# Packing tokens for the experts: the 24 rows of the third token tile in two row groups and two banks

## The chip, the cores and the metric

The kernel runs on one core of a Trainium2 chip. The metric is the device time of one execution in microseconds (us); several executions are timed and their median is given.

## The reference

One inference step of a two-layer decoder trunk for a prompt of 272 tokens (16 learned ones and 256 given) and 8 sample tokens, together 280 tokens of 1024 features. Each layer has a mixer (layer 0: retention beside a state space model; layer 1: RWKV-7 beside latent attention), a normalisation, and then a mixture of 16 experts in 4 groups, each with 256 hidden features. All is float32. What the change touches is the mixture:

```
coarse = softmax(x @ w_coarse + b)            # 4 groups, the best one is taken
fine   = logits of that group's 4 experts      # the best two are taken
y      = sum over the two experts e of  weight_e * (silu(x @ gate_e) * (x @ up_e)) @ down_e
```

Each token is so sent to 2 of 16 experts.

## The kernel before, in words

The activations lie feature-major in `XT` (128 partitions, 8 feature blocks, 280 tokens). Tokens are cut into three tiles `TT`: 128, 128 and 24 rows.

Per layer `out_and_moe` (TensorE) does: the output projection, the normalisation sums, the router logits (line 1588), then a transposition of `XT` to token-major form (line 1596), which ScalarE copies from the banks to `XTM` (line 2178). `XTM` has three tiles of 128 rows; of the third only 24 rows hold tokens, and GpSimd clears the whole third tile beforehand (`rest_zero`, line 1154), for which ScalarE waits.

Meanwhile VectorE works out the picks: `PICK` is a token by expert table of zeros and ones (lines 2002 and 2004; the second signals `pick_ready`). TensorE multiplies it by a table of "row before column" (`before`, lines 1602 to 1607), so that each token gets its place in its expert's list of at most 64. VectorE turns that into `PLACE` (line 2009) and, for one group of experts at a time, into `DSP` (line 2015), a token by slot table of zeros and ones, by comparison with `iota`. `dispatch_ready` counts the groups.

Then come eight pairs of experts (`q` from 0 to 7). `pack(q, half)` (line 1612) gathers the tokens of the pair: for four feature blocks, and for each of three token tiles, one product of `XTM` (stationary, 128 tokens by 128 features) with `DSP` (moving, 128 tokens by 128 slots), summed in one bank of four blocks of 128 columns. VectorE copies the bank to `XG` (`packed`, line 2018). `gate_or_up` (line 1630) multiplies `XG` by the weights, two experts side by side in the two 64-column halves of the array. `weights_turned` (line 1640) transposes the weighted dispatch table, its third part with 24 rows. `hidden_turned` (line 1648) transposes the hidden features, `down` (line 1662) multiplies them by the last weights.

The order is written out by hand. Two packs come ahead of the first pair. For each pair: gate, up, `pack(q + 1, 0)`, `weights_turned(q - 1)`, `hidden_turned(q)`, `pack(q + 1, 1)`, `down(q)`. The weights come through SyncE's DMA queue, 1 MB each, into nine buffers. After the last pair, line 1690 sums the experts' outputs into the residual.

Banks: VectorE empties four banks (`V`), ScalarE the other four (`A`), each a ring. `claim` waits until the bank was emptied, `take` waits until it was filled, `close` signals it full. `s.do` waits for the instruction's own completion before the engine goes on. ScalarE's order in `moe` (line 2172) is: normalisation, the six copies to `XTM`, an exponential (line 2180, waits for `lc_shift`), another (line 2182, waits for `lf_diff`), then the activations of the pairs.

Of the kernel before, what the change touches and what calls it, by code (L numbers as in the profile page):

```python
# [27 lines left out]
P = 128  # L28
D = 1024
KD = D // P  # L30
# [27 lines left out]
CAP = 64  # L58
# [6 lines left out]
          ("retmask", RH * NPR), ("kdec", 3 * RH), ("gam", 1), ("selbh", NB * RH),  # L65
          ("strictT", P), ("inclT", P), ("m2T", P), ("m2N", P),
          ("off2", P), ("off4", P), ("off8", P), ("off16", P),
          ("scan", NPR), ("causal", P), ("curmask", 2 * NB), ("rank", 4), ("eps", 4), ("before", P), ("iota", CAP)]
COFF = {}
_o = 0  # L70
for _n, _w in CONSTS:
# [5 lines left out]
def const_table():  # L77
    c = {n: np.zeros((P, w), np.float64) for n, w in CONSTS}
    i = np.arange(P)
    c["ident"] = np.eye(P)  # L80
    c["ones"][:] = 1.0
    c["id64"] = (i[:, None] % 64 == np.arange(64)[None, :]).astype(float)
    c["blk"] = (i[:, None] // 64 == i[None, :] // 64).astype(float)
    for name, d in (("perm64", 64), ("perm32", 32)):
        for m in range(P):
            if m % d < d // 2:
                c[name][m + d // 2, m] = -1.0
            else:
                c[name][m - d // 2, m] = 1.0
    pos = np.concatenate([np.arange(NPR), np.full(NB, PAST)]).astype(np.float32)  # L90
    for d, names in ((64, ("cosd", "sind")), (32, ("cosr", "sinr"))):
        inv = (10000.0 ** (-np.arange(0, d, 2, dtype=np.float32) / np.float32(d))).astype(np.float32)
        ang = (pos[None, :] * inv[:, None]).astype(np.float32)[i % (d // 2)]
        c[names[0]], c[names[1]] = np.cos(ang.astype(np.float64)), np.sin(ang.astype(np.float64))
    logg = np.log1p(-np.exp2(-5.0 - np.arange(RH)))
    x = np.arange(NPR)
    diff = x[None, :] - i[:, None]
    c["retmask"] = np.concatenate([np.where(diff >= 0, np.exp(logg[h] * np.maximum(diff, 0)), 0.0) for h in range(RH)], 1)
    c["kdec"] = np.stack([np.exp(logg[h] * np.maximum(NPR - 1 - (128 * t + i), 0)) for t in range(3) for h in range(RH)], 1)
    h_of = (i // 4) % RH  # L100
    c["gam"] = np.exp(logg[h_of])[:, None]
    c["selbh"] = ((i[:, None] // 4 // RH == np.arange(RH * NB)[None, :] % NB) &
                  (h_of[:, None] == np.arange(RH * NB)[None, :] // NB)).astype(float)
    a, b = i[:, None], i[None, :]
    blk = a // WC == b // WC
    c["strictT"] = (blk & (a < b)).astype(float)
    c["inclT"] = (blk & (a <= b)).astype(float)
    c["m2T"] = ((a // 2 == b // 2) & (a < b)).astype(float)
    c["m2N"] = ((a // 2 == b // 2) & (b < a)).astype(float)
    for s in (2, 4, 8, 16):  # L110
        c[f"off{s}"] = ((a // (2 * s) == b // (2 * s)) & (a // s > b // s)).astype(float)
    c["scan"] = np.broadcast_to((x % WC != 0).astype(float), (P, NPR))
    c["causal"] = np.where(b <= a, 0.0, -BIG)
    c["curmask"] = np.where(i[:, None] // 32 + 4 * (np.arange(2 * NB)[None, :] // NB) == np.arange(2 * NB)[None, :] % NB, 0.0, -BIG)
    c["rank"] = np.broadcast_to(np.array([4.0, 3.0, 2.0, 1.0]), (P, 4))
    c["eps"] = np.broadcast_to(np.array([1e-5, 64e-5, 1e-6, 0.0]), (P, 4))
    c["before"] = (a < b).astype(float)
    c["iota"] = np.broadcast_to(np.arange(1, CAP + 1)[None, :].astype(float), (P, CAP))
    return np.ascontiguousarray(np.concatenate([c[n] for n, _ in CONSTS], 1).astype(np.float32))

# [97 lines left out]
def program(nc, a, outs):  # L218
    sems = {}

    with ExitStack() as ctx:
# [6 lines left out]
        def ev(name):  # L228

            if name not in sems:  # L230
                sems[name] = sem(name)
            return sems[name]
# [21 lines left out]
        def cst(name):  # L254
            o, w = COFF[name]
            return CST[:, o:o + w]
# [74 lines left out]
        SIL, HB, HT = part(0, 2, DE), part(512, 2, DE), part(1024, 2, 2, P)  # L331
        LG, RT = part(1536, 3, 20), part(1600, 10, 3, 16)
        PICK, COMB, PLACE, CNT = part(2080, 3, NE), part(2128, 3, NE), part(2176, 3, NE), part(2224, NE)
        XTM = part(2240, 3, KD, P)
        XG = part(5312, 2, KD, P)
        DSP = part(7360, 3, NE, CAP)
        DSPT = part(10432, NQ, NT)
# [807 lines left out]
        def odd_pool(pool, s):  # L1145
# [2 lines left out]
                pool.wait_ge(ev("ln_done"), KD * (2 * l + 1))  # L1148
                pool.tensor_scalar(RES[:, :, :], XT[:, :, :], ALPHA, None, ALU.mult).then_inc(ev("sum_start"), 1)

            def rest_zero(l):

                pool.wait_ge(*mark[f"out{l}"])
                pool.memset(XTM[:, 2], 0.0).then_inc(ev("rest_zero"), 1)

            def weighted(l):

                pool.wait_ge(ev("comb_ready"), l + 1)
# [12 lines left out]
                s.do(pool.tensor_tensor(dst, TS[:, :, 0], TS[:, :, 1], ALU.add), sem)  # L1171


            rest_zero(0)
            weighted(0)
            sum_start(0)

# [37 lines left out]
            for sm in range(NB):  # L1215
                for pg in range(NPG):
# [1 line left out]
                    if i >= EARLY_PAGES:  # L1218
                        page.append(pool.value_load(PTAB[0:1, i:i + 1], min_val=0, max_val=a["cache_krope"].shape[0] - 1))
                    pool.dma_start(CK[:, sm, pg, 256:288], a["cache_krope"][bass.ds(page[i], 1), 0].rearrange("o p c -> p (o c)")).then_inc(ev(f"cache_krope_in{sm}"), 16)  # L1220
            rest_zero(1)
            weighted(1)
            sum_start(1)

# [45 lines left out]
        def _(pe):  # L1270
# [275 lines left out]
            def out_and_moe(l, s_out):  # L1546
# [55 lines left out]
                for t, (c0, r) in enumerate(TT):  # L1602
                    for u in range(t):
                        pe.matmul(b[:, NE * t:NE * t + NE], cst("ones"), one(u), start=(u == 0), stop=False)
                    pe.matmul(b[:, NE * t:NE * t + NE], cst("before")[:r, :], one(t), start=(t == 0), stop=True)
                for t, (c0, r) in enumerate(TT):
                    ins = pe.matmul(b[:, 3 * NE:4 * NE], cst("ones")[:r, :], one(t), start=(t == 0), stop=(t == 2))
                close(V, ins, "places")
# [3 lines left out]
                def pack(q, half):  # L1612

                    pe.wait_ge(ev("dispatch_ready"), NG * l + q // 2 + 1)
                    b = V.claim()
                    for i in range(4):
                        for t in range(3):
                            ins = pe.matmul(b[:, P * i:P * i + P], XTM[:, t, 4 * half + i, :], DSP[:, t, 2 * q:2 * q + 2, :].rearrange("p e c -> p (e c)"),  # L1618
                                            start=(t == 0), stop=(t == 2))
                    close(V, ins, f"xg{l}")  # L1620

                def gate_or_up(q, ring, n, name):

# [76 lines left out]
        def _(dve):  # L1700
# [266 lines left out]
            def out_and_moe(l):  # L1967
# [37 lines left out]
                dve.wait_ge(dve_step, s.n[dve_step.name])  # L2005
                s.do(sub(r1[5], r1[4], r1[3]), ev("lf_diff"))

                b = V.take()
                s.do(dve.scalar_tensor_tensor(PLACE, b[:, 0:3 * NE].rearrange("p (t e) -> p t e", t=3), 1.0, PICK, ALU.add, ALU.mult))
                s.do(dve.tensor_copy(CNT, b[:, 3 * NE:4 * NE]), v_free)  # L2010
# [5 lines left out]
                    s.mark(ins, ev("dispatch_ready"))  # L2016

                def packed(q, half):
                    empty(XG[:, q % 2, 4 * half:4 * half + 4, :], 512)

                dispatch(0)
                s.do(dve.tensor_reduce(CNT[:, 0:1], CNT, AX.X, ALU.max))
# [66 lines left out]
        def _(act):  # L2089
# [81 lines left out]

            def moe(l):
                layer_norm(2 * l, "ln1_g", "ln1_b", l)
                act.wait_ge(ev("rest_zero"), l + 1)
                for t, (c0, r) in enumerate(TT):
                    for h in range(2):
                        b = A.take()
                        act.activation(XTM[:r, t, :, 64 * h:64 * h + 64], b[:r, 0:512].rearrange("r (p k) -> r k p", k=KD), ACT.Copy).then_inc(a_free, 1)
                act.wait_ge(ev("lc_shift"), l + 1)
                act.activation(RT[:, 2, :, 0:4], RT[:, 2, :, 0:4], ACT.Exp).then_inc(ev("lc_exp"), 1)  # L2180
                act.wait_ge(ev("lf_diff"), l + 1)
                act.activation(RT[:, 5, :, 8:9], RT[:, 5, :, 8:9], ACT.Exp).then_inc(ev("lc_exp"), 1)
                for q in range(NQ):
# [155 lines left out]
```

## Time and profile before

| | us |
|---|---|
| median of 3 runs | 1191.88 (1188.89 to 1192.0) |
| profiled execution | 1186.78 |
| its span | 1185.1 |
| TensorE busy, matmuls | 1011.8 |
| VectorE busy | 495.1 |
| ScalarE busy | 202.6 |

The profile is of one execution. A busy matmul row overlaps with its neighbours, because matmuls are pipelined: each of them lasts some 0.28 us, while the next one starts 0.11 us after it. Weight loads (PEld) run beside matmuls. A product of two float32 operands shows as two loads and two matmuls.

### The profile page before, as it was taken

The page shows a single profiled execution, that of the slowest core. Times are in us where ns is not written, and L with a number is a line of the kernel's source. Part 1 is how long each engine was busy: PE and PEld are TensorE (multiplying, and loading weights), DVE is VectorE, ACT ScalarE, POOL GpSimd, SP SyncE. Part 2 cuts the span into 40 slices and gives each one's busy share as a digit, 9 for nine tenths or more (in the row PEclk, how much of TensorE's full clock was granted, in tenths as well). Part 3 has the DMA queues.
Part 4 walks back from the last instruction along what each step waited for, and adds up shares of the span by engine and source line. Part 5 has one row for each costly group of instructions (what it writes and reads, how often), then busy time and mean ns, then how long its engine had stood idle before and what let it go on. Part 6 is the DMA issues. An engine that isn't in the chain of part 4 may idle for free.

```text
span 1185.1 us, 17689 instructions
## 1 busy us (share of the span) xinstructions
PE 1011.8 (85%) x7132; PEld 766.8 (65%) x7132; DVE 495.1 (42%) x1056; ACT 202.6 (17%) x418; POOL 139.8 (12%) x179
## 2 busy tenths in 40 slices
PE   6998477778999999899747778889888888999995
PEld 4785365556867667688537678755455667667674
DVE  1796723453411111321587575584753235111104
ACT  0121001202210110301510000013355032110103
POOL 0004001000130000000026800000730002200000
PEclk9995756789799999999868889688599987999998
DMA  9402202525099994152000000010731541999501
GB/s 313 168 2 27 41 1 76 221 72 217 4 355 389 372 361 138 37 142 76 2 10 1 38 2 3 2 41 21 226 87 47 199 181 40 357 385 373 232 1 37
DMA packets 77203, 156.81 MB, mean 132 GB/s; under 512 B 19596, under 2 KB 57539, under 8 KB 68196
## 3 DMA queue, kind: packets, MB, share of 16 engines
q1 hardware_dynamic: 67650, 148.28, 34.4%
q0 software_dynamic: 3760, 4.48, 1.7%
q10 hardware_dynamic: 5710, 2.90, 0.9%
q8 instruction: 58, 0.95, 0.3%
q14 instruction: 25, 0.20, 0.1%
HBM read 149.18 MB, written 5.27 MB: 130 GB/s over the span
## 4 chain that ended last, share of the span: by engine, by line
PE 72%; DVE 21%; issue 2%; ACT 2%; DMA 2%; SPq 0%; DVEq 0%
PE bank L1630 9%; PE bank L1304 9%; PE bank L1618 8%; DVE scratch L1714 8%; PE bank L1690 5%; PE bank L1662 5%; PE bank L1557 5%; DVE scratch L1717 2%; PE bank L1418 2%; PE bank L1365 2%; PE bank L558 2%; PE bank L744 2%; PE bank L1588 2%; PE bank L1506 1%; PE bank L569 1%
## 5 line engine op out<-in xcount | busy, mean ns | idle before, releaser
L1304 PE MATMUL bank<-x_fm,weight_slots 128*128 128x280 f32 x576 | 140.9, 408 | 3.4 <-ACT x_fm L2170 2.8
L1304 PEld LDWEIGHTS bank<-x_fm,weight_slots 128*128 128x128 f32 x576 | 111.8, 195 | 31.0 <-issue 2.9
L2102 ACT ACTIVATE scratch<-bank 128x280 f32<-128x280 f32 (+5 forms) x136 | 60.9, 454 | 398.8 <-PE bank L1304 110.8
L1711 DVE COPY scratch<-bank 128x512 f32<-128x512 f32 (+5 forms) x92 | 57.6, 627 | 100.3 <-PE bank L1618 73.1
L1618 PE MATMUL bank<-scratch 128*128 128x128 f32 x768 | 95.8, 283 | 3.5 <-issue 3.5
L1618 PEld LDWEIGHTS bank<-scratch 128*128 128x128 f32 x768 | 91.6, 198 | 9.0 <-issue 9.0
L1630 PE MATMUL bank<-weight_slots,scratch 128*64 128x256 f32 x672 | 92.5, 379 | 1.7 <-DVE scratch L1711 1.7
L1630 PEld LDWEIGHTS bank<-weight_slots,scratch 128*64 128x64 f32 x672 | 58.6, 137 | 28.2 <-issue 4.6
L1714 DVE TENSOR_TENSOR scratch<-bank,scratch 128x256 f32<-128x256 f32 (+1 forms) x20 | 8.6, 430 | 141.2 <-PE bank L1630 140.6
L1557 PE MATMUL bank<-scratch,weight_slots 128*128 128x280 f32 x256 | 63.3, 410 | 4.9 <-DVE scratch L1714 4.9
L1714 DVE TENSOR_TENSOR scratch<-scratch 128x64 f32<-128x64 f32 (+13 forms) x97 | 60.4, 641 | 15.5 <-ACT scratch L2102 13.0
L1690 PE MATMUL bank<-scratch 128*128 128x280 f32 x256 | 60.9, 400 | 1.4 <-ACT scratch L2102 1.4
L1557 PEld LDWEIGHTS bank<-scratch,weight_slots 128*128 128x128 f32 x256 | 50.0, 196 | 17.6 <-DVE scratch L1714 5.3
L1690 PEld LDWEIGHTS bank<-scratch 128*128 128x128 f32 x256 | 48.5, 190 | 14.7 <-ACT scratch L2102 3.2
L1630 PE MATMUL bank<-scratch 128*64 128x256 f32 x352 | 56.9, 379 | 0.0
L1220 POOL DMA_DIRECT2D scratch<-in_cache_krope x64 | 34.3, 536 | 162.9 <-DVE residual L994 145.5
L1630 PEld LDWEIGHTS bank<-scratch 128*64 128x64 f32 x352 | 35.7, 137 | 16.4 <-issue 3.4
L1662 PE MATMUL bank<-weight_slots,scratch 128*64 128x512 f32 x192 | 43.8, 598 | 0.3
L1418 PE MATMUL bank<-scratch 64*42 64x128 f32 x128 | 25.9, 418 | 18.9 <-DVE scratch L1717 18.9
L1714 DVE TENSOR_TENSOR scratch<-bank,consts 128x512 f32<-128x512 f32 (+5 forms) x69 | 33.7, 488 | 14.9 <-PE bank L558 11.7
L2163 ACT ACTIVATE scratch<-residual 128x280 f32<-128x280 f32 x32 | 11.7, 437 | 157.4 <-DVE residual L1960 157.4
L1490 PE MATMUL bank<-scratch,consts 128*128 128x280 f32 x58 | 21.5, 540 | 18.8 <-DVE scratch L1714 17.8
(370 smaller groups left out, 1467.5 us busy)
## 6 DMA issues: line engine op xcount, KB each, us to landing
weight_slots<-in_moe_w_down SPq DMA_DIRECT2D x24, 1024.0 KB, 8.9
weight_slots<-in_moe_w_up SPq DMA_DIRECT2D x22, 1024.0 KB, 7.5
weight_slots<-in_moe_w_gate SPq DMA_DIRECT2D x20, 1024.0 KB, 6.2
scratch<-in_moe_w_gate SPq DMA_DIRECT2D x12, 1024.0 KB, 8.1
scratch<-in_moe_w_up SPq DMA_DIRECT2D x10, 1024.0 KB, 8.1
weight_slots<-in_od_w_in SPq DMA_DIRECT2D x9, 1024.0 KB, 5.3
weight_slots<-in_ev_w_in SPq DMA_DIRECT2D x8, 1024.0 KB, 11.6
scratch<-in_moe_w_down SPq DMA_DIRECT2D x8, 1024.0 KB, 9.4
```

The source lines that it names most:

```text
L558: ins = pe.matmul(heads(b, r)[:r, hp, :], NTM[:r, par, hp, 0:r], TM_[:r, par, hp, 0:r], start=True, stop=True)
L1220: pool.dma_start(CK[:, sm, pg, 256:288], a["cache_krope"][bass.ds(page[i], 1), 0].rearrange("o p c -> p (o c)")).then_inc(ev(f"cache_krope ...
L1304: ins = pe.matmul(b[:, 0:NT], w[:, k, P * m2:P * m2 + P], src[:, k, :], start=(k == 0), stop=(k == kt - 1))
L1418: ins = pe.matmul(b[0:HCOL, P * i:P * i + P], HS[lo:lo + SP_N, j, g // 2, :], CP[lo:lo + SP_N, j, g // 2, 1:CL + 1, :].rearrange("p l c -> ...
L1557: ins = pe.matmul(b[:, 0:NT], w[:, k0 + k, P * m2:P * m2 + P], src[:, k, :], start=(which == 0 and k == 0), stop=(which == 1 and k == 3))
L1618: ins = pe.matmul(b[:, P * i:P * i + P], XTM[:, t, 4 * half + i, :], DSP[:, t, 2 * q:2 * q + 2, :].rearrange("p e c -> p (e c)"), start=(t ...
L1630: ins = pe.matmul(b[CAP * j:CAP * j + CAP, 0:DE], XG[:, q % 2, k, CAP * j:CAP * j + CAP], w[j][:, k, :], start=(k == 0), stop=(k == KD - 1))
L1662: ins = pe.matmul(b[CAP * j:CAP * j + CAP, :], HT[:, q % 2, f, CAP * j:CAP * j + CAP], w[j][:, f, 512 * h:512 * h + 512], start=(f == 0), ...
L1690: ins = pe.matmul(b[:, 0:NT], YG[:, q, P * m:P * m + P], DSPT[:, q, :], start=(q == 0), stop=(q == NQ - 1))
L1711: s.do(dve.tensor_copy(dst, src if len(dst.shape) == 2 else src.rearrange("p (a b) -> p a b", a=dst.shape[1])), v_free)
L1714: return dve.tensor_tensor(o, x, y, ALU.mult)
L2102: return act.activation(dst, b[:rows, 0:width], f, **kw).then_inc(a_free, 1)
```

## The change

The third tile's 24 rows now lie twice, in partitions 0 to 23 and 32 to 55, in `XTM3`: the first copy holds two of each four feature blocks, the second the other two. `pack` claims two banks, and two 24-row products (one per row group, one per bank) start the sums; the four 128-row products of the two banks follow. `PICK` is copied to partitions 32 to 55, the constant table `before32` gives their places, and VectorE waits for that copy (`pick_spread`) before it computes `PLACE`. `packed` empties two banks of 256 columns. The clearing by GpSimd is gone.

```diff
     c["before"] = (a < b).astype(float)
+    c["before32"] = (a < b % 32).astype(float)
...
-        XTM = part(2240, 3, KD, P)
+        XTM, XTM3 = part(2240, 2, KD, P), part(4288, 2, 2, P)
...
-            def rest_zero(l):
-
-                pool.wait_ge(*mark[f"out{l}"])
-                pool.memset(XTM[:, 2], 0.0).then_inc(ev("rest_zero"), 1)
...
-                    pe.matmul(b[:, NE * t:NE * t + NE], cst("before")[:r, :], one(t), start=(t == 0), stop=True)
+                    pe.matmul(b[:, NE * t:NE * t + NE], cst("before32" if t == 2 else "before")[:r, :], one(t), start=(t == 0), stop=True)
...
-                    b = V.claim()
-                    for i in range(4):
-                        for t in range(3):
-                            ins = pe.matmul(b[:, P * i:P * i + P], XTM[:, t, 4 * half + i, :], DSP[:, t, 2 * q:2 * q + 2, :].rearrange("p e c -> p (e c)"),
-                                            start=(t == 0), stop=(t == 2))
-                    close(V, ins, f"xg{l}")
+                    b = [V.claim(), V.claim()]
+                    slots = lambda t, rows: DSP[rows, t, 2 * q:2 * q + 2, :].rearrange("p e c -> p (e c)")
+                    for i in range(2):
+                        for c in range(2):
+                            rows = slice(32 * c, 32 * c + TT[2][1])
+                            pe.matmul(b[c][:, P * i:P * i + P], XTM3[rows, half, i, :], slots(2, rows), start=True, stop=False)
+                        ins = []
+                        for c in range(2):
+                            for t in range(2):
+                                last = pe.matmul(b[c][:, P * i:P * i + P], XTM[:, t, 4 * half + 2 * c + i, :], slots(t, slice(0, P)), start=False, stop=(t == 1))
+                            ins.append(last)
+                    for c in range(2):
+                        close(V, ins[c], f"xg{l}")
...
+                dve.wait_ge(ev("pick_spread"), l + 1)
                 b = V.take()
...
-                    empty(XG[:, q % 2, 4 * half:4 * half + 4, :], 512)
+                    for c in range(2):
+                        k = 4 * half + 2 * c
+                        empty(XG[:, q % 2, k:k + 2, :], 2 * P)
...
-                act.wait_ge(ev("rest_zero"), l + 1)
...
-                        act.activation(XTM[:r, t, :, 64 * h:64 * h + 64], b[:r, 0:512].rearrange("r (p k) -> r k p", k=KD), ACT.Copy).then_inc(a_free, 1)
+                        if t < 2:
+                            act.activation(XTM[:r, t, :, 64 * h:64 * h + 64], b[:r, 0:512].rearrange("r (p k) -> r k p", k=KD), ACT.Copy).then_inc(a_free, 1)
+                        else:
+                            for c in range(2):
+                                ins = act.activation(XTM3[32 * c:32 * c + r, :, :, 64 * h:64 * h + 64],
+                                                     b[:r, 0:512].rearrange("r (p half c i) -> r c half i p", half=2, c=2, i=2)[:, c], ACT.Copy)
+                            ins.then_inc(a_free, 1)
...
                 act.activation(RT[:, 2, :, 0:4], RT[:, 2, :, 0:4], ACT.Exp).then_inc(ev("lc_exp"), 1)
+                act.wait_ge(ev("pick_ready"), l + 1)
+                act.activation(PICK[32:32 + TT[2][1], 2, :], PICK[0:TT[2][1], 2, :], ACT.Copy).then_inc(ev("pick_spread"), 1)
                 act.wait_ge(ev("lf_diff"), l + 1)
```

## Rows read from the trace of the kernel before

**Rows 1.** The page: span, and TensorE's busy time, share, instructions.

```profile
span 1185.1 us, 17689 instructions
...
PE 1011.8 (85%) x7132; PEld 766.8 (65%) x7132; DVE 495.1 (42%) x1056; ACT 202.6 (17%) x418; POOL 139.8 (12%) x179
```

**Rows 2.** The page, part 4: the chain that ended last, by engine and line.

```profile
PE 72%; DVE 21%; issue 2%; ACT 2%; DMA 2%; SPq 0%; DVEq 0%
PE bank L1630 9%; PE bank L1304 9%; PE bank L1618 8%; DVE scratch L1714 8%; PE bank L1690 5%; PE bank L1662 5%; PE bank L1557 5%; DVE scratch L1717 2%; PE bank L1418 2%; PE bank L1365 2%; PE bank L558 2%; PE bank L744 2%; PE bank L1588 2%; PE bank L1506 1%; PE bank L569 1%
```

**Rows 3.** The chain in order of time, layer 0: start, length, what.

```profile
312.76 7.03 PE bank L1618 x48
...
319.88 0.70 DVE scratch L1711
...
344.02 2.88 PE bank L1618 x24
346.90 0.39 PE bank L1640 x3
347.28 0.37 PE bank L1648 x2
347.65 2.68 PE bank L1618 x24
350.33 3.58 PE bank L1662 x16
353.91 6.91 PE bank L1630 x64
```

**Rows 4.** Windows: length, busy (count) by engine, granted clock, DMA share, GB/s.

```profile
312.70:315.70 3.00, 2.94 (x14) 2.97 (x15) 1.29 (x5) 0.00 (x0) 0.00 (x0) 0.50 0.00 0
...
360.82:377.62 16.80, 16.80 (x134) 11.65 (x134) 2.23 (x4) 1.99 (x4) 0.00 (x0) 1.00 0.93 374
```

**Rows 5.** Timeline at a pack's head: start, length, engine, line, operation, shapes, idle.

```profile
360.44 0.38 PE L1630 MATMUL bank<-scratch 128*64 128x256 f32 x1
360.75 0.41 PEld L1618 LDWEIGHTS bank<-scratch 128*128 128x128 f32 x3 [0.39 <-issue]
360.75 0.49 PE L1618 MATMUL bank<-scratch 128*128 128x128 f32 x2
```

**Rows 6.** Timeline of the weight loads in the place sums.

```profile
309.19 0.53 PEld L1604 LDWEIGHTS bank<-scratch,consts 128*128 128x128 f32 x4
309.75 0.29 PEld L1605 LDWEIGHTS bank<-scratch,consts 24*128 24x128 f32 x2
310.07 0.84 PEld L1607 LDWEIGHTS bank<-scratch,consts 128*128 128x128 f32 x6
```

**Rows 7.** Timeline of a group of 64-row products in two row groups.

```profile
621.89 1.16 PE L546 MATMUL bank<-scratch 64*128 64x128 f32 x16 [0.77 <-DVE scratch L1714]
```

**Rows 8.** Groups by form: busy us, mean ns, idle before with releasers.

```profile
L1711 DVE COPY scratch<-bank 128x512 f32<-128x512 f32 x56 | 38.7, 691 | 90.3 <-PE bank L1618 73.1 <-PE bank L692 7.0 <-PE bank L582 4.4
...
L1711 DVE COPY scratch<-bank 128x256 f32<-128x256 f32 x18 | 7.6, 425 | 3.1 <-PE bank L1648 1.5
...
L2102 ACT ACTIVATE scratch<-bank 128x256 f32<-128x256 f32 x16 | 6.2, 385 | 65.7 <-PE bank L1630 65.7
...
L602 PE MATMUL bank<-scratch 32*64 32x64 f32 x384 | 4.7, 232 | 3.3 <-DVE scratch L1717 1.9 <-issue 1.4
```

**Rows 9.** Timelines of ScalarE and VectorE around the place sums.

```profile
308.62 0.59 ACT L2178 ACTIVATE scratch<-bank 24x512 f32<-24x512 f32 x1 [0.27 <-PE bank L1596]
309.23 1.28 ACT L2180 ACT_TABLE_LOAD   x1
...
310.64 0.19 ACT L2182 ACTIVATE scratch<-scratch 128x3 f32<-128x3 f32 x1
...
311.11 0.21 DVE L2009 SCALAR_TENSOR_TENSOR scratch<-bank,scratch 128x48 f32<-128x48 f32 x1 [2.88 <-PE bank L1607]
```

**Rows 10.** Timeline of GpSimd, 230 to 309 us.

```profile
282.33 0.95 POOL L1154 MEMSET scratch<- 128x1024 f32 x1 [78.74 <-DVE residual L1970]
```

**Rows 11.** DMA issues, first 100 us: size, time to landing.

```profile
consts<-in_consts ACTq DMA_DIRECT2D x1, 2234.5 KB, 9.0
```

More of the change, by code:

```diff
@@ L67 @@
           ("off2", P), ("off4", P), ("off8", P), ("off16", P),
-          ("scan", NPR), ("causal", P), ("curmask", 2 * NB), ("rank", 4), ("eps", 4), ("before", P), ("iota", CAP)]
+          ("scan", NPR), ("causal", P), ("curmask", 2 * NB), ("rank", 4), ("eps", 4), ("before", P), ("before32", P), ("iota", CAP)]
 COFF = {}
@@ L1171, in row_sums @@
                 s.do(pool.tensor_tensor(dst, TS[:, :, 0], TS[:, :, 1], ALU.add), sem)
-            rest_zero(0)
             weighted(0)
@@ L1220, in odd_pool @@
                     pool.dma_start(CK[:, sm, pg, 256:288], a["cache_krope"][bass.ds(page[i], 1), 0].rearrange("o p c -> p (o c)")).then_inc(ev(f"cache_krope_in{sm}"), 16)
-            rest_zero(1)
             weighted(1)
```

## The prediction, made before the changed kernel was built or run

> **What bounds the kernel now.** I read the totals first [rows 1]: TensorE is busy 85% of a span of 1185.1 us; the profiled execution took 1186.78 us. Then the chain of waits by share [rows 2]: 72% of it is TensorE, and line 1618, the product that the change rewrites, is 8% of the span, some 95 us. The chain in order of time [rows 3] shows one expert pair of the mixture after the other with nothing between: pack 2.88, three transposes 0.39, two transposes 0.37, pack 2.68, down 3.58, gate and up 6.91 us, which is 16.80 us per pair. In the windows view [rows 4] that period has 16.80 us of TensorE in 16.80 us, at the full granted clock (1.00, the 2.4 GHz level). The weight stream is close behind: the DMA engines are busy 93% of the period. So in these periods each nanosecond added to or taken from TensorE's stream moves the end, except that a gain is capped at 7% of a period, 1.2 us, by the weights. There are 32 packs, 16 per layer: two ahead of the first pair, then for each of the 7 following pairs one right behind gate and up (call it A) and one behind the transposes (B).
>
> **What one pack costs.** A pack is 12 products, each of which is issued as two weight load and matmul pairs: 24 instructions. Pack B takes 2.68 us for x24 [rows 3], so a slot is 0.1117 us. Pack A has the same 24 instructions and takes 2.88 us. The difference stands at its head [rows 5]: the last matmul of gate and up is on 64-column tiles and starts at 360.44; it streams for some 0.21 us, yet the first load of the pack starts at 360.75, and the load engine was idle 0.39 us; then one load lies bare before the second matmul. So a change of tile shape costs 2.88 - 2.68 = 0.20 us: about 0.1 for letting the array run empty and about 0.1 for a load of 128 columns that no matmul covers.
>
> Is that also so for a change between 128 rows and 24 rows? The trace has it twice with 24 rows. The place sums [rows 6]: four full loads at 309.19, the two 24-row loads at 309.75, full loads again at 310.07. Four slots should take 0.45, they take 0.56; two slots should take 0.22, they take 0.32. That is 0.11 and 0.10 per change, with 16 moving columns, behind which a bare load hardly shows. And the transposes in rows 3: 0.39 + 0.37 us for five, of which the third has 24 rows and streams 24 columns; four full slots are 0.45 and the short one at most 0.06, so two changes cost about 0.25. Bounds of a change: 0.10 (place sums) and 0.20 (head of pack A). The new products stream 128 columns and load 128, as pack A does, so I take 0.195.
>
> **What the change removes.** Of each pack's 12 products the four of the third tile become four products of 24 rows, two and two side by side in the row groups 0 and 32. Do two row groups run together? The trace before has such a pair in line 546 (64 rows, 128 columns, two row groups, two banks): 16 instructions in 1.16 us [rows 7]. Without its bare first load and its tail of 0.27 that is 8 slots of 0.11, not 16. And line 602 with 32 rows: x384 in 4.7 us busy [rows 8], 12 ns each, many tiles at once. So I take a pair at its full worth: 8 instructions take 4 slots, and a pack loses 4 x 0.1117 = 0.447 us. Over 32 packs that is -14.3 us. The lower bound of the gain is nothing: pairs one after the other.
>
> **What it adds on TensorE.** The order in a pack is now: small pair, eight full instructions, small pair, eight full. Inside there are three changes of shape (24 to 128, 128 to 24, 24 to 128). At the head, pack A had a change already (64 columns to 128, now 64 columns to 24 rows); pack B came in the same shape and now has a fourth. The two packs ahead of the first pair: the first starts from rest, three; the second follows a full one, four.
> - 14 packs A: 3 x 0.195 - 0.447 = +0.138 each, +1.9.
> - 14 packs B: 4 x 0.195 - 0.447 = +0.333 each, +4.7.
> - 2 second packs: +0.333 each, +0.7.
> - 2 first packs: mostly at half clock (the first 3.0 us after the wait are granted 0.50, the 1.2 GHz level [rows 4]), so twice 0.138, +0.55 for both.
> Sum +7.9 us. There are 42 + 56 + 8 + 6 = 112 changes; by the bounds of one change it is 112 x 0.10 - 14.3 = -3.1 and 112 x 0.20 - 14.3 = +8.1.
>
> The Trainium skill would have it otherwise: TensorE: Matmul & The Clock Gate, "Part 2: What happens when you issue a matmul", says that weight loads are pulled ahead of running matmuls when the row groups don't conflict or the load goes to the background buffer. By that rule the bare load would vanish and a change would cost the drain alone; that is the first rival below. Rows 5 show a load that waited for the array to be empty, against it.
>
> **What it adds elsewhere.**
> - VectorE empties two banks of 256 columns in place of one of 512: 2 x 0.425 for 0.691 us [rows 8]. In the periods VectorE is busy 2.23 of 16.80 us [rows 4], so that is free, and the first half now closes four slots earlier. The ring of four banks is claimed six times per pair, not four. The tightest claim is pack B's second bank, which needs pack A's first: that bank is full 0.45 us before pack A ends and is emptied in 0.43, while the transposes give another 0.76; no wait. Ahead of the first pair, where the chain goes through the copy of 0.70 us [rows 3], only the second half of 0.425 is left: -0.27 per layer, -0.5.
> - ScalarE moves the third tile in four smaller operations in place of two: at the end two of at most 0.385 [rows 8] for one of 0.59 [rows 9], +0.1 to +0.2 us. Behind it stand the table load of 1.28 and the exponentials, and now the new copy of the picks (24x16, at most 0.2 us), for which VectorE waits before it computes the places. It would end at about 310.85 + 0.15 + 0.1 = 311.1; VectorE starts line 2009 at 311.11 now, behind the place sums. So the cover is exactly used up: between 0 and 0.2 per layer, I take +0.1 for both. That a copy needs no table of its own shows in rows 9: the transposed tiles are copied right up to the load, which the exponential brings.
> - POOL's memset of 0.95 us ran from 282.33 [rows 10], 26 us before the last copy into its tile; its removal is worth nothing. The 128 new constant columns are 64 KB on a transfer of 2234.5 KB in 9.0 us [rows 11], 0.26 us, early beside the projections; nothing.
>
> Total: +7.9 - 0.5 + 0.1 = +7.5 us on 1186.78, 1194.3 for such an execution. The median of the three runs shown, 1191.88, lies 5.1 above the profiled one; the same step on it gives 1199.4.
>
> **The rivals.**
> 1. A change of shape costs the drain alone (0.10). Place: the head of every run of full or small instructions. Then 11.2 - 14.3 - 0.4 = -3.5 us: 1188.4. It decides from 14.7 / 112 = 0.131 us per change downward. For it: rows 6. Against it: rows 6 stream 16 columns, where the drain is all that can show, and rows 5 and the 2.88 against 2.68 are with real widths. Chance 0.13.
> 2. The pairs don't run side by side at every head, since each product is two instructions and the group has only two products: three slots or four in place of two. Then 64 pairs give back 0.11 or 0.22 each, 7 to 14 us: 1206.5 to 1213.7. For it: no row has groups of only two products. Against it: line 546 starts in step. Chance 0.08.
> 3. The new wait for the copied picks reaches the chain, because the copy does call for a table load of 1.28 us: two layers, +2.6 to +5 us on top: 1202 to 1204. Against it: rows 9. Chance 0.05.
> 4. The weights are the true bound (DMA busy 93%), and part of a slower TensorE is hidden: half of the step, 1195.5. Against it: no DMA in the chain of the periods. Chance 0.06.
> My forecast has 0.68.
>
> **How the numbers follow.** 0.3% is 3.6 us, about what a measurement here can tell from no change. The forecast's own range, with a change between 0.17 and 0.21 us and the spread of 3 us in the runs of before, is 1194 to 1203. Slower by over 0.3% (over 1195.5): nine tenths of the forecast (the rest is what the spread of the runs can take from it), rivals 2 and 3, and half of 4, together 0.77. Rival 1 is at the edge of faster, -3.5 us: half of it and a little for what I overlook, 0.08. The rest, 0.15, is no difference. For 8 in 10 the range takes the low end down to 1191, and the high end to the start of rival 2, 1207.
>
> **What would show it.** In the chain, the period of a pair goes from 16.80 to about 17.27 us, pack A from 2.88 to 3.0 and pack B from 2.68 to 3.0; the 24-row loads come in two pairs with the starts of a pair under 0.04 us apart; ahead of each group of loads there is an idle stretch of TensorE's load engine; the DMA share in the periods falls from 0.93 to about 0.91; the mean slot of the remaining full instructions stays 0.11. Rival 1 shows as a period below 16.7, rival 2 as small loads one slot apart, rival 3 as a table load between the exponentials and a later start of line 2009 than its place sums allow. I am wrong if the period doesn't grow.

## The result: 1205.72 us against 1191.94, slower as forecast, but by about twice as much

| | before | changed |
|---|---|---|
| median | 1191.94 us (4 runs) | 1205.72 us (4 runs, 1202.75 to 1207.65) |
| ratio | | 1.0132, 95% interval 1.0084 to 1.018 |
| profiled execution, span | 1186.78, 1185.1 us | 1207.65, 1206.0 us |

The forecast was 1199.4 us, +7.5; the time is inside the range of 1191 to 1207, the step is not of the forecast size: +13.8 by the medians, 1.8 times what was forecast. (The two medians alone give a ratio of 1.0116; the ratio on record, 1.0132, lies above it, and its interval holds both.) On two more occasions the changed kernel came to 1.0093 (1.006 to 1.0126) and 1.0131 (1.0096 to 1.0166). The kernel before against itself gave 1.0002 (0.9976 to 1.0028).

The page of the changed kernel: the packs are now lines 1614 (24 rows) and 1618 (128 rows), 2% + 6% of the chain; they were 8% [rows 2].

```profile
PE 1032.1 (86%) x7132; PEld 768.9 (64%) x7132; DVE 499.4 (41%) x1088; ACT 204.3 (17%) x424; POOL 138.0 (11%) x177
...
PE bank L1631 9%; PE bank L1298 9%; DVE scratch L1715 7%; PE bank L1618 6%; PE bank L1691 5%; PE bank L1663 5%; PE bank L1551 5%; PE bank L1614 2%; DVE scratch L1718 2%; PE bank L1412 2%; PE bank L559 2%; PE bank L1359 2%; PE bank L745 2%; PE bank L1582 2%; PE bank L1484 2%
```

The chain in order of time, layer 0 (start, length, what). First the packs ahead of the first pair, then one period in the middle (the lines left out are marked):

```profile
310.87 2.23 issue
313.10 0.80 PE bank L1614 x4
313.89 2.00 PE bank L1618 x8
...
322.09 2.02 PE bank L1618 x8
...
324.68 9.10 PE bank L1631 x64
...
343.63 6.91 PE bank L1631 x64
350.54 0.42 PE bank L1614 x4
350.96 1.09 PE bank L1618 x8
...
353.55 0.39 PE bank L1641 x3
...
357.32 3.58 PE bank L1663 x16
360.91 6.91 PE bank L1631 x64
```

The period is 360.91 - 343.63 = 17.28 us, for 16.80 in rows 3; forecast was 17.27. A pack is 2 x (0.42 + 1.09) = 3.02 us; forecast 3.0. In the timeline of a pack's head (four neighbours are merged into one row) the small loads start two and two: within a pair 0.01 us apart, at 367.74, and the second pair 0.11 us behind, at 367.85. So four small instructions take two slots, and the idle stretch ahead of the loads is there:

```profile
367.43 0.38 PE L1631 MATMUL bank<-scratch 128*64 128x256 f32 x1
367.74 0.30 PEld L1614 LDWEIGHTS bank<-scratch 24*128 24x128 f32 x4 [0.39 <-issue]
367.74 0.49 PE L1614 MATMUL bank<-scratch 24*128 24x128 f32 x4
...
368.16 0.97 PEld L1618 LDWEIGHTS bank<-scratch 128*128 128x128 f32 x8
```

What the forecast did not have stands ahead of the first period. 313.10 to 324.68 is 11.58 us for the two packs and VectorE's last copy, where the kernel before has 7.87 (312.76 [rows 3] to 320.63); gate and up behind them 9.10 us, not 6.91 or 7.13. The lengths of the single pieces, 0.73 for 0.42 and 2.00 for 1.09, are those of half clock, and the windows say so (length, busy and count of PE, PEld, DVE, ACT, POOL, granted clock, DMA share, GB/s):

```profile
313.10:315.90 2.80, 2.80 (x14) 2.35 (x14) 1.25 (x4) 0.00 (x0) 0.00 (x0) 0.50 0.01 3
...
318.60:321.30 2.70, 2.70 (x14) 2.25 (x13) 1.12 (x5) 0.00 (x0) 0.00 (x0) 0.50 0.00 0
...
324.70:327.00 2.30, 2.30 (x12) 1.35 (x14) 2.10 (x8) 0.00 (x0) 1.03 (x2) 0.50 0.00 0
327.00:329.00 2.00, 2.00 (x14) 1.16 (x12) 2.00 (x4) 0.00 (x0) 2.00 (x3) 0.57 0.00 0
329.00:331.00 2.00, 2.00 (x22) 1.27 (x20) 1.11 (x2) 0.39 (x1) 2.00 (x4) 1.00 0.00 0
...
360.90:378.20 17.30, 17.30 (x136) 11.24 (x133) 2.54 (x6) 1.99 (x4) 0.00 (x0) 1.00 0.91 364
```

TensorE is busy without a gap, and yet the half clock (the 1.2 GHz level) lasts some 15 us from the first pack on; before, it was 0.50 for 3.0 us of the packs and then full [rows 4]. In layer 1 it is the same: 11.6 us for 8.55, then 8.50 for 7.13.

Stage by stage, from the starts of TensorE's instructions, in two traces of the kernel before (the second is e12) and three of the changed one (the page's, e5, e11). Where a cell has a slash, layer 0 stands ahead of it and layer 1 behind; a step is the difference of the means, both layers together:

| stage, us | before | changed | step | forecast |
|---|---|---|---|---|
| place sums to first pack, layer 0 / 1 | 4.10, 3.99 / 4.20, 4.24 | 4.47, 4.22, 4.47 / 4.33, 4.34, 4.35 | +0.5 | +0.1 |
| first two packs and copy, layer 0 / 1 | 7.87, 9.20 / 8.55, 8.51 | 11.59 in all | +6.1 | +0.7 |
| first gate and up, to its last start, layer 0 / 1 | 6.75 in all | 8.72, 7.43, 8.60 / 8.12, 8.11, 8.10 | +2.9 | 0 |
| the rest of the eight pairs, each layer | 123.33 | 126.69 | +6.7 | +6.6 |
| between the two mixtures | 535.7, 540.6 | 539.4, 538.1, 539.3 | none beyond the spread | 0 |
| sum | | | +16.2 | +7.4 |

Whole executions moved by less than the +16.2 of the stages on two of the three occasions: +13.8, +10.9 (e5) and +16.2 (e11) by the medians, and +14.2 by the mean spans of the five traces. The difference lies in stretches that the change does not touch, above all the one ahead of the first place sums, which took 304.9 to 310.2 us in these five traces.

### The profile page after: what moved, and what is told of

Read it like the earlier page. It is cut to its first block, busy times and chain, and to the rows that moved or that the text cites. A ratio compares the mean times of both kernels' runs of the same rounds, so it can differ in the third digit from the quotient of the medians.

```text
span 1206.0 us, 17757 instructions
## 1 busy us (share of the span) xinstructions
PE 1032.1 (86%) x7132; PEld 768.9 (64%) x7132; DVE 499.4 (41%) x1088; ACT 204.3 (17%) x424; POOL 138.0 (11%) x177
## 4 chain that ended last, share of the span: by engine, by line
PE 73%; DVE 21%; issue 2%; ACT 2%; DMA 2%; SPq 0%; DVEq 0%
PE bank L1631 9%; PE bank L1298 9%; DVE scratch L1715 7%; PE bank L1618 6%; PE bank L1691 5%; PE bank L1663 5%; PE bank L1551 5%; PE bank L1614 2%; DVE scratch L1718 2%; PE bank L1412 2%; PE bank L559 2%; PE bank L1359 2%; PE bank L745 2%; PE bank L1582 2%; PE bank L1484 2%
## 5 line engine op out<-in xcount | busy, mean ns | idle before, releaser
L1712 DVE COPY scratch<-bank 128x256 f32<-128x256 f32 (+5 forms) x124 | 62.7, 505 | 106.5 <-PE bank L1618 74.2
L1631 PE MATMUL bank<-weight_slots,scratch 128*64 128x256 f32 x672 | 95.9, 391 | 1.2 <-DVE scratch L1712 1.2
L1618 PE MATMUL bank<-scratch 128*128 128x128 f32 x512 | 81.5, 307 | 0.0
L1618 PEld LDWEIGHTS bank<-scratch 128*128 128x128 f32 x512 | 68.4, 208 | 8.6 <-issue 1.8
L1551 PEld LDWEIGHTS bank<-scratch,weight_slots 128*128 128x128 f32 x256 | 50.4, 198 | 16.9 <-DVE scratch L1715 4.2
L1691 PEld LDWEIGHTS bank<-scratch 128*128 128x128 f32 x256 | 48.5, 190 | 14.7 <-ACT scratch L2106 3.2
L1631 PEld LDWEIGHTS bank<-scratch 128*64 128x64 f32 x352 | 35.7, 137 | 16.4 <-issue 3.4
L1159 POOL TENSOR_TENSOR scratch<-scratch 128x256 f32<-128x256 f32 x24 | 16.1, 704 | 250.8 <-DVE scratch L1715 250.8
```

The lines of the kernel that those rows point to most:

```text
L1551: ins = pe.matmul(b[:, 0:NT], w[:, k0 + k, P * m2:P * m2 + P], src[:, k, :], start=(which == 0 and k == 0), stop=(which == 1 and k == 3))
L1618: last = pe.matmul(b[c][:, P * i:P * i + P], XTM[:, t, 4 * half + 2 * c + i, :], slots(t, slice(0, P)), start=False, stop=(t == 1))
L1631: ins = pe.matmul(b[CAP * j:CAP * j + CAP, 0:DE], XG[:, q % 2, k, CAP * j:CAP * j + CAP], w[j][:, k, :], start=(k == 0), stop=(k == KD - 1))
L1691: ins = pe.matmul(b[:, 0:NT], YG[:, q, P * m:P * m + P], DSPT[:, q, :], start=(q == 0), stop=(q == NQ - 1))
L1712: s.do(dve.tensor_copy(dst, src if len(dst.shape) == 2 else src.rearrange("p (a b) -> p a b", a=dst.shape[1])), v_free)
```

## The experiments

**e1 and e10, the first two packs as before.** All other packs as changed. (Each cut of an edit is marked by three dots.)

```diff
...
-                pack(0, 0)
-                pack(0, 1)
+                pack_plain(0, 0)
+                pack_plain(0, 1)
...
```

`pack_plain` is the pack of the kernel before: one bank, zero-padded third tile.

> The changed kernel, but the two packs ahead of the first expert pair are made as before (zero-padded third tile, one bank, 24 full instructions each); ScalarE's extra copies for it come behind its exponentials, GpSimd's clearing is back. Theory (the clock): in the changed kernel the packs ahead of the first pair ran wholly at the half clock, and the stream of drains and short groups is what keeps the clock down. Then the first packs take about 7.0 to 7.7 us as before (changed: 11.0), the first gate and up 7.1 (changed: 9.1 and 8.5), the later periods stay at 17.27, and the kernel is 10 to 11 us faster than the changed one: 5 to 7 us over the one before, ratio 1.005. Rival (a longer rest ahead of the packs, 2.2 in place of 1.8 us, from the wait for the copied picks, sets the clock): the rest is unchanged here, so the first packs would stay at the half clock, some 10.3 us for 48 instructions, and the kernel at +13 to +15.

> e1 once more, beside the changed kernel on the same chip. Theory (the clock in the first packs and the gate and up behind them costs the changed kernel 8 to 10 us): 8 us under the changed kernel of this call, ratio 1.005 to the one before. Rival (what the first packs lose in clock comes back elsewhere in the kernel, so that only the periods count): within 3 us of the changed kernel.

Measured: 1.0083 (1.0055 to 1.0111) and 1.008 (1.0053 to 1.0107) of the kernel before; the changed kernel beside e10 1.0131. The medians of that call, 1199.64 and 1206.28 us, are 6.6 apart. By stage the layer 0 packs with their copy took 8.91 and 9.24 us and those of layer 1 7.78 and 7.80, gate and up 6.75 in all four cases, the rest 126.69. The clock came up 2.8 to 5.9 us after the start of the packs in all four cases; in the three traces of the changed kernel it never came up before they ended. So the stream of the first packs sets the clock, and the rival (the longer rest ahead of them) falls: the rest was 2.2 us in e1's layer 0, as in the changed kernel. The windows of e1, over the first packs of layer 0:

```profile
313.45:317.60 4.15, 4.15 (x19) 4.15 (x20) 1.25 (x4) 0.75 (x1) 0.00 (x0) 0.50 0.00 0
317.60:321.50 3.90, 3.90 (x31) 3.72 (x29) 1.39 (x5) 0.00 (x0) 0.00 (x0) 0.87 0.00 0
```

By the stages it should have been 9 us under the changed kernel (10 to 11 were expected), not 6.6; the stretch between the mixtures took 541.9 and 542.2 us in its two traces, the longest of all. Its time goes with the clock: of that stretch 160 us are at half clock in both traces, 154 to 157 in the three of the changed kernel, which is worth about 2 to 3 us (see e12). Whether these two kernels meet more of it by chance stays open.

**e2, stand-in products in the rest ahead of the packs.**

```diff
...
+                for i in range(8):
+                    pe.matmul(banks_next()[:, 0:P], XTM[:, 0, i % KD, :], XTM[:, 1, i % KD, :], start=True, stop=True)
                 pack(0, 0)
...
```

> The changed kernel with 8 additional products of 128x128 by 128 columns (16 instructions, results thrown away: they go to the bank that the first pack overwrites) in the rest between the place sums and the first pack, about 1.8 us at the full clock, 3.4 at half. Theory (the clock): where the clock is full at the end of the place sums (layer 0) it stays so, the four small groups and first packs take 6.0 instead of 11.0 us and gate and up 6.9 instead of 9.1: -7 us there. In layer 1 the clock falls within the place sums; the products either lift it (-6.6) or lie at half clock and delay the packs by 1.6 (0 to +1.6). In all 5 to 14 us faster than the changed kernel. Rival (the extra time of the first packs is not the clock's but the banks' or VectorE's): no change or +1.6 per layer.

Measured: 1.013 (1.0075 to 1.0186), no gain in all, where 5 to 14 us had been expected. The chain and windows show why: in layer 0 the stand-ins took 3.12 us, the clock came up 0.9 us behind their end, and the same packs that had stayed at half clock now ran at the full one (the third window), gate and up in 7.13. In layer 1 it did not come up: stand-ins 3.71, each piece at half clock, gate and up 9.26.

```profile
312.50:315.60 3.10, 3.10 (x18) 2.88 (x18) 2.41 (x10) 1.92 (x4) 0.00 (x0) 0.59 0.01 3
315.60:317.50 1.90, 1.90 (x14) 1.56 (x14) 0.40 (x2) 0.00 (x0) 0.00 (x0) 0.77 0.00 0
317.50:321.60 4.10, 4.10 (x35) 3.50 (x35) 1.54 (x6) 0.00 (x0) 0.00 (x0) 1.00 0.00 0
```

```profile
996.65 3.71 PE bank L1671 x16
1000.36 0.73 PE bank L1616 x4
...
1011.88 9.26 PE bank L1633 x64
```

So neither the banks nor VectorE make the first packs long; the same instructions take 0.42 + 1.09 with the clock up and 0.73 + 2.00 without. In these traces the changed packs keep a clock that is up, but do not bring it up. Why the same stand-ins were followed by a full clock in layer 0 and not in layer 1 is not shown.

**e3, no pair side by side.**

```diff
...
-                            rows = slice(32 * c, 32 * c + TT[2][1])
-                            pe.matmul(b[c][:, P * i:P * i + P], XTM3[rows, half, i, :], slots(2, rows), start=True, stop=False)
+                            rows = slice(0, TT[2][1])
+                            pe.matmul(b[c][:, P * i:P * i + P], XTM3[rows, c, half, i, :], slots(2, rows), start=True, stop=False)
...
```

> The changed kernel with both 24-row products of a group in row group 0, so that they can't run side by side; the number of changes of tile shape is the same. Theory (a pair is worth two slots of 0.1117 us): a small group takes 0.64 instead of 0.42 us, a period of an expert pair 17.27 + 4 x 0.223 = 18.17 us, the kernel about 12.5 us slower than the changed one in the periods alone. Rival (the drain, not the row groups, sets the length of a small group): the period stays at 17.3. On the clock: if the short groups are what keeps it down, more instructions in them may lift it earlier than in the changed kernel; if the drains are, it stays at half for the first packs.

Measured: one time of 1209.31 us. The chain:

```profile
347.30 0.64 PE bank L1614 x4
347.93 1.09 PE bank L1618 x8
```

0.64 for 0.42 is the two slots of 0.11 us, as the working had it; the seven periods took 132.74 for 126.69 us, 0.86 each (0.89 expected). The rival falls. The clock stayed at half through the first packs, here 13.24 us with the copy: more instructions in the groups did not lift it. The whole kernel was only 3.6 us over the changed kernel's median of 1205.72, where 12.5 had been expected: by stages the two mixtures took 13.6 us more than in the changed kernel's first trace, and the stretches outside them 12 us less in this single execution (303.7 us ahead of the first place sums, 532 between the mixtures).

**e4, the small products of a pack together.**

```diff
...
+                def pack_small(q, half):
...
+                    pe.wait_ge(ev("dispatch_ready"), NG * l + q // 2 + 1)
+                    b = [V.claim(), V.claim()]
+                    for i in range(2):
+                        for c in range(2):
+                            rows = slice(32 * c, 32 * c + TT[2][1])
+                            pe.matmul(b[c][:, P * i:P * i + P], XTM3[rows, half, i, :], slots(q, 2, rows), start=(i == 0), stop=False, skip_group_check=True)
+                    return b
+
+                def pack_full(q, half, b):
...
+                    for c in range(2):
+                        for i in range(2):
+                            for t in range(2):
+                                ins = pe.matmul(b[c][:, P * i:P * i + P], XTM[:, t, 4 * half + 2 * c + i, :], slots(q, t, slice(0, P)), start=False, stop=(t == 1), skip_group_check=True)
+                        close(V, ins, f"xg{l}")
...
```

> The changed kernel with the order in a pack altered: all four 24-row products first, then the 16 full instructions, bank 0 before bank 1. Two changes of shape per pack less: 112 - 64 = 48 remain. Theory (0.195 us per change, as predicted and as the chain shows): pack A goes from 3.02 to 2.63 us, pack B likewise, a period from 17.27 to 16.49 us, below the 16.80 of before; seven periods and the packs bring -12.5 us against the changed kernel at the full clock. With the longer plain run of 16 instructions the clock may also come up sooner in the first packs: up to -10 more. So between -0.5% and +0.3% of the kernel before if the clock stays down, down to -1% if it comes up. Rival (a change costs the drain alone and the rest of the loss lies in the two banks): the period falls by 0.4 at most, to 16.9.

Measured: 0.9961 (0.9934 to 0.9988), faster than both. The chain:

```profile
339.74 6.91 PE bank L1638 x64
346.65 0.64 PE bank L1613 x8
347.29 1.98 PE bank L1621 x16
349.27 0.39 PE bank L1648 x3
...
356.24 6.91 PE bank L1638 x64
```

The period (356.24 - 339.74) is 16.50 us, where 16.49 was worked out: four changes of shape fewer, 0.78 us less, 0.195 each. That measures the price between products of 128 columns, and the rival (the drain alone, and the rest in the banks) falls: it needed 16.9. The first packs with the copy took 10.32 and 8.09 us: in layer 0 the clock came up only 9.5 us after their start, as they ended, in layer 1 after 4.7 us.

**e5 and e11, the changed kernel again.** Unaltered, no diff.

> The changed kernel once more, unaltered, on the chip of the runs below, to have its time against theirs. Both theories: a ratio of 1.012 to 1.016 to the kernel before.

> The changed kernel, unaltered, beside e10. Both: 1.009 to 1.014 of the kernel before.

Measured: 1.0093 (e5) and 1.0131 (e11); e5 is below what was expected.

**e6, changes of shape in the kernel before.**

```diff
...
                     for i in range(4):
+                        if q == 0:
+                            pe.matmul(b[:, P * i:P * i + 16], XTM[:24, 0, i, :], XTM[:24, 1, i, 0:16], start=True, stop=True)
                         for t in range(3):
...
```

> The kernel before, with one 24-row product of 16 columns put ahead of each of the four sums in the two packs ahead of the first pair (8 per layer, their results are overwritten). The full work of those packs stays, 48 full instructions; what is added is a change of tile shape and back, eight times. Theory A (the drains at the changes keep the clock down): the two packs stay at half clock to the end, 16 to 18 us in place of 7.0 and 7.7, and the first gate and up takes over 7.5. Theory B (fewer rows or columns per time, as the 24-row products stream, keep it down; drains don't): the clock comes up 3 to 5 us into the packs as before, and they take 11 to 13 us, gate and up 7.1.

Measured: 1.0153 (1.011 to 1.0195). The two packs took 17.0 us in each layer, and the windows are at half clock to their end and beyond; gate and up 9.53 and 8.81 us.

```profile
314.00:318.00 4.00, 3.96 (x16) 3.69 (x16) 1.26 (x5) 0.00 (x0) 0.00 (x0) 0.50 0.00 2
...
326.00:331.00 5.00, 4.98 (x20) 4.16 (x19) 0.00 (x0) 0.00 (x0) 0.00 (x0) 0.50 0.00 0
...
336.00:339.00 3.00, 3.00 (x26) 1.86 (x24) 1.26 (x2) 0.39 (x1) 3.00 (x6) 0.88 0.13 19
```

Nothing of the change is in this kernel but the changes of shape, and it shows the changed kernel's picture. Theory A's times came, theory B's did not. Not told apart: whether it is the emptying of the array as such, or the share of time that it and the short products take from the stream, since the added product brings both.

**e7, all small products of the first two packs ahead, and the picks copied before the exponential.**

```diff
...
-                pack(0, 0)
-                pack(0, 1)
+                small = [pack_small(0, half) for half in range(2)]
+                for half in range(2):
+                    pack_full(0, half, small[half])
...
```

The functions are those of e4; ScalarE's copy of the picks moves ahead of its first exponential.

> The grouped order (all four small products of a pack ahead of its 16 full instructions), and two alterations: in the packs ahead of the first pair all eight small products come first, so that 32 full instructions follow without a change of shape; and ScalarE copies the picks before its first exponential, not after it. Theory A (drains keep the clock down): the clock comes up some 4 to 6 us into these packs, which then take 7 to 8 us in place of the 9.8 of the grouped order; VectorE starts the places behind the place sums, 0.1 us after them. Period 16.49 as in the grouped order. In all 5 to 8 us under the kernel before, ratio 0.993 to 0.996. Theory B: no sooner than in the grouped order; 3 to 4 us under.

Measured: 0.997 (0.9944 to 0.9995). The first packs and the copy took 8.12 and 9.10 us, within 0.6 of the first trace of before. The clock came up 5.6 us after their start in layer 0 and 7.6 in layer 1, where they started at 994.12:

```profile
316.00:319.20 3.20, 3.20 (x17) 3.20 (x17) 0.42 (x1) 0.00 (x0) 0.00 (x0) 0.52 0.00 0
319.30:321.60 2.30, 1.75 (x16) 1.55 (x14) 1.97 (x7) 0.00 (x0) 0.00 (x0) 1.00 0.00 0
...
997.00:1001.70 4.70, 4.70 (x24) 4.70 (x24) 1.54 (x6) 0.00 (x0) 0.00 (x0) 0.50 0.00 0
```

VectorE's places no longer wait for the copy. In the changed kernel (first block of rows) ScalarE's copy at 311.15 released them; in e7 (second block) TensorE's sums did:

```profile
308.06 1.54 ACT L2185 ACTIVATE scratch<-bank 24x256 f32<-24x256 f32 x4 [0.26 <-PE bank L1590]
...
311.15 0.21 ACT L2191 ACTIVATE scratch<-scratch 24x16 f32<-24x16 f32 x1
...
311.45 0.21 DVE L2011 SCALAR_TENSOR_TENSOR scratch<-bank,scratch 128x48 f32<-128x48 f32 x1 [2.92 <-ACT scratch L2191]
```

```profile
311.86 0.21 DVE L2019 SCALAR_TENSOR_TENSOR scratch<-bank,scratch 128x48 f32<-128x48 f32 x1 [2.47 <-PE bank L1601]
```

Against e4 the whole kernel did not get measurably faster. It was 3.0 us under the kernel before by the medians, where theory A expected 5 to 8 and theory B 3 to 4, and the clock came up earlier than in e4 in layer 0 (5.6 for 9.5 us) and later in layer 1 (7.6 for 4.7). So this run does not decide between the two theories; what it shows is that the wait for the copy is gone.

**e8 and e9, pack B's small products beside the 24-row transposition.**

```diff
...
+                        turned = V.claim()
+                        small = pack_small(q + 1, 1)
+                        hidden_turned(q, turned)
+                        mark[f"ht{l}"] = (v_free, V.n - 2)
+                        pack_full(q + 1, 1, small)
...
```

The line with `mark` stands in e9 alone. In both the rest is as in e7.

> As e7, and pack B's four small products stand right behind the 24-row transposition of line 1640's successor, whose tile shape they share, ahead of the two transposes of the hidden features; so pack B adds no change of shape. At 0.195 us per change the period falls from 16.49 to 16.10 us, 12 times over: 4.7 us under e7, ratio 0.989 to 0.992. Rival (the weights bound it): the DMA engines were busy 93% of 16.80 us, that is 15.6 us of work per period; if they cannot be filled above 0.95, the period stops at 16.4 and TensorE or its load engine waits for a weight slot.

> As e8, but down waits for the copy of the hidden features alone; in e8 its wait counted the two banks of pack B as well, since they had been claimed before it was set, and it stood 0.53 us per period behind VectorE's copies of pack B. Theory: the period goes from 16.85 to 16.2 us (6.91 + 0.64 + 1.98 + 0.39 + 0.53 + 0.37 + 1.80 + 3.58), 8 us less than e8 over 14 periods; ratio 0.989 to 0.993 to the kernel before. Rival (the weights): 15.6 us of transfers per period allow no less than some 16.4, and waits for a weight slot appear.

Measured: e8 0.9962 (0.9936 to 0.9988), e9 0.9881 (0.9854 to 0.9907), 1176.77 us, the fastest of all. The expected ranges were 0.989 to 0.992 for e8, which missed it, and 0.989 to 0.993 for e9, which came out a little faster. In e8 the changes of shape were gone, but down stood behind VectorE's copies of pack B, and the period was 16.85 us, not 16.10; I had not seen that the wait counts banks in the order in which they are claimed. The chain of e8, then that of e9:

```profile
348.65 1.80 PE bank L1621 x16
...
350.54 0.44 DVE scratch L1723
```

```profile
361.65 0.64 PE bank L1613 x8
362.30 1.98 PE bank L1621 x16
364.28 0.39 PE bank L1648 x3
364.66 0.53 PE bank L1613 x8
365.20 0.37 PE bank L1656 x2
365.56 1.79 PE bank L1621 x16
367.35 3.59 PE bank L1670 x16
```

With its own wait the period is 16.2 us as worked out from the pieces of e8. Against the 16.50 us of e4 two changes of shape are gone for 0.30 us, 0.15 each and not 0.195; so beside the transpositions, the short one of which streams 24 columns, a change cost less. The weights did not stop it, and the rival's floor of 16.4 us did not hold: the DMA engines are now busy 97% of it, and no wait for a slot stands in the chain.

```profile
360.00:376.20 16.20, 16.20 (x137) 10.86 (x135) 2.54 (x6) 1.98 (x4) 0.00 (x0) 1.00 0.97 387
```

**e12, the kernel before against itself.**

> The kernel before, unaltered, against itself: the comparison's own error, and a second trace of it. Open is whether the stretch between the two mixtures (from the end of layer 0's pairs to layer 1's place sums), 535.7 us in the trace of before and 538.1 to 539.4 in three traces of the changed kernel, differs by what the change does. Theory (it is the spread of that stretch, in which neither kernel's instructions differ): the second trace has 538 to 542. Rival (the change lengthens it by some 3 us): the second trace has 535 to 536 again. Ratio 0.997 to 1.003.

Measured: 1.0002 (0.9976 to 1.0028). The stretch between the mixtures took 540.6 us in this trace, 535.7 in the first, with the same instructions. So the +3.7 of the changed kernel's first trace in that stretch is within what one kernel shows. Where the 4.9 us between the two traces of before lie can be read from the granted clock: 157 us of the stretch are at half clock in e12, 147 in the first trace, and where TensorE sets the pace 10 us at half instead of full clock cost 5. One part of it, the same 26 us from the stretch's start in both, first in the trace of before, then in e12:

```profile
902.70:928.70 26.00, 22.77 (x273) 14.80 (x273) 6.68 (x14) 8.07 (x17) 0.00 (x0) 0.93 0.47 163
```

```profile
905.70:931.70 26.00, 22.75 (x209) 14.53 (x213) 6.83 (x18) 8.43 (x17) 0.00 (x0) 0.80 0.36 121
```

TensorE does 273 matmuls in it at a clock of 0.93, and 209 at 0.80.

## Why the prediction was half right

**The mechanism and its price: right.** 0.195 us per change of shape, two slots of 0.1117 us per pair, period 17.27 forecast and 17.28 measured; e3 and e4 measured both terms apart. Only beside the 24-column transposition the price was too high (0.15 in e9), as the smaller figures of the prediction for the place sums and the transposes suggested. For the 28 packs of the periods +6.6 us was forecast and +6.7 came.

**The first packs: this step failed.** The prediction put them at "mostly at half clock ... so twice 0.138, +0.55 for both", plus 0.67 for the second ones and less 0.5 for the shorter copy. That took over from the trace of before that the clock comes up 3.0 us after the start, as if it were a fixed delay. It hangs on what TensorE does: with seven or more changes of shape inside the two packs it stayed at 0.50 to the end of them (changed kernel, e3, e6), without any it came up 2.8 to 5.9 us after their start (before, e12, e1, e10). Between the two lie e4 (9.5 and 4.7 us, three changes) and e7 (5.6 and 7.6, one). So the delay of the trace of before was not even fixed for the same kernel: 3.0 us there, 5.8 in e12. The packs and copies cost +6.1 us where +0.7 was expected.

**Gate and up behind them: a term that was missing.** Costed at nothing, it took +2.9 us, since the half clock lasts into it. With what the packs cost beyond the forecast, 5.4 us, that is 8.3 of the 8.8 us that the forecast was short by the stages (6.3 by the medians), and both stand where the clock was down.

**The wait for the copied picks: right place, a size off.** +0.1 was taken, with up to 0.4 allowed; it was about +0.5 for both layers. The four small copies of the third tile end at 309.60, the two before ended at 309.21 [rows 9], and everything on ScalarE behind them, the table load, the exponential and the copy of the picks, is later by that.

**The range.** That 1205.72 us lies inside it is luck. The forecast's own part ended at 1203; the end at 1207 was set by rival 2, pairs that do not run side by side, and that did not come.

**The rivals.** 1 (drain alone) is refuted by e4. 2 (pairs one after the other) is refuted by the timeline and e3. 3 (a table load for the copy) did not come: the loads are the two of before. 4 (the weights hide part) is refuted by the period of 17.28, and by e9, whose period is shorter than the one of before with the same weights.

Of the rule of the Trainium skill that weight loads are pulled ahead of running matmuls (TensorE: Matmul & The Clock Gate, Part 2): the trace agrees within one tile shape, where a slot is 0.11 us with the load hidden, and differs at a change of shape: at a pack's head the load starts 0.31 us after the start of the last matmul before it (367.74 for 367.43), though a slot of that matmul is 0.21 us, and the load engine is idle for 0.39 us. That it waits for the array to be empty is the reading that fits; the trace does not show the array itself.

## What to carry to other kernels

Count the changes of tile shape before packing small products: one costs 0.195 us here at the full clock, a pair side by side earns 0.22 us, so a single pair between two full runs loses; group the small products, or put them beside others of the same shape (e9: 1.2% faster than the kernel before). Where a stage starts from rest at half clock, the time until the clock comes up is no constant to take over from the old trace: changes in the stream can stretch it over the whole stage and into the next. And a wait that counts banks must be read again when the order of claims changes.

## What was not expected of the hardware

A stream that leaves the clock up where it is up need not bring it up: the changed packs ran at 1.00 in the periods and in e2's layer 0 (4.1 us in the window shown), and at 0.50 for 11 us when they began there. Whether they would keep it for longer is not shown. TensorE's busy share was 100% in both, so it says nothing on this. And the same stretch of 536 to 541 us differed by 5 us between two executions of one kernel, by the time that it ran at half clock.
